# A transformer-like block on one core: keys projected first, diagonal blocks stored by eight small transfers, the delta rule and the attention part moved to earlier places, a new order at the start

## The chip, the cores and the metric

The kernel runs on one core of a Trainium2 chip. The metric is the device time of one execution in microseconds (us); less is better. The time before is the median of three runs, 1259.57 us (1257.01 to 1261.92). The core has five engines that run their own instruction streams and wait for each other by semaphores: TensorE (PE, matrix multiplications), VectorE (DVE), ScalarE (ACT, functions from tables), GpSimd (POOL) and SyncE (SP, which here only issues DMA transfers). ACT issues some transfers too.

## The reference, cut to what matters

One layer for 256 tokens of width 2048, all float32. The token mixer projects the normalised input with one weight, then runs eight heads of stick-breaking attention and eight heads of gated delta rule side by side (head width 128), and projects the result back. A gated MLP with a causal convolution follows. Of the mixer the change touches the order of nearly all steps:

```python
xn = rmsnorm(x, ln_mix_pre)
proj = xn @ w_in                       # sb q,k,v | dn q,k,v | dn z | dn b,a
# stick-breaking, per head and block of 128 queries
z = q @ k.T * 128**-0.5                # log_sigmoid of z and -z, masked
att = exp(log_beta + later)            # later: reversed cumulative sum of log_1m
o_sb = rmsnorm(att @ v, sb_out_gain)
# delta rule, per head; chunks of 64 in the reference
q, k, v = silu(causal_conv4(dn_qkv))   # q and k then l2-normalised
L = where(strict, (k * beta) @ k.T * decay, 0)
T_mat = inverse(I + L)                 # triangular
u, w = T_mat @ (v * beta), T_mat @ (k * beta * exp(g))
# per chunk: v_new = u - w @ S; o = q*exp(g) @ S + qk @ v_new; S = S*exp(g_last) + k.T @ v_new
o_dn = rmsnorm(o_dn, dn_out_gain) * silu(dn_z)
h = x + rmsnorm(concat(o_sb, o_dn) @ w_out, ln_mix_post)
y = h + rmsnorm(conv_ffn(rmsnorm(h, ln_ffn_pre)), ln_ffn_post)
```

## The kernel before, in words

**Precision and weights.** Each float32 weight is split in two parts that PE can take at full speed: `w_hi` (rounded, by ACT, L464) and `w_lo` (the remainder, by DVE, L891); the activations are held in the same two parts (`xhl`, `mix_hl`, `ffn_act`). A product is hi x hi and lo, and lo x hi. Weights come as chunks of 1 MB (`raw`, four slots), issued by SP; a chunk has four pieces of 128x512, and `w_hi` and `w_lo` are rings of eight pieces. A split is made six pieces ahead of PE's use (AHEAD). So ACT and DVE may lag by about six pieces before PE has nothing to do.

**Places.** The input projection is 14 groups of 16 pieces. The first ten give features (`tile_piece`, four tiles of 128 features by 256 tokens, banks 0 to 3); the last four give tokens (`token_piece`). The number of a piece in this order, 0 to 223, is a place. Every engine has a function `follow(place)` that does its share of the stream up to that place: PE the pieces, ACT the splits, the copies of the lower half of a bank (`halves`), the first tap of the convolution and its silu, DVE the splits, the bank additions (`added`) and three taps for each conv tile, POOL the token scale (L346), SP the chunk loads. All other work of the mixer is hung on that stream: the table PLACE gives each step a place, and each engine calls `follow` up to it, then waits for its semaphores and does the step. An engine that waits there makes no splits meanwhile. The program order of each engine is fixed by this.

**The head.** SP loads x in four quarters, each followed by one chunk. ACT issues the gains and four small tensors, then rounds four k-blocks of x (L535), splits the first four pieces, and so on; DVE does the remainders (L934). ACT asks for `xcopy` (x by tokens, 2 MB) after split 5, squares it (L563), takes the root at place 11; DVE makes two diagonals of it (L960) that PE sums at place 14 (L1398) to a scale for each token. At 9 to 12 PE projects the gate columns (`ba`, L1391); DVE, ACT and PE form decays from them at places 15 to 27, and SP stores them and loads them spread over partitions (`dm`).

**Delta rule.** Two batches of four heads, `for b in range(BATCHES)`, hang from places 44 and 115. Keys are turned and their norms taken; `low` is the scaled triangular system in `ltri` (L1028). The diagonal 16x16 blocks are inverted row by row: POOL masks `ltri` to its diagonal blocks (L396), DVE reduces them to `packed` (L1040), SP stores that (64 KB, runs of 512 B for each partition), ACT loads it spread over partitions (`block_l`, L613) at place 58, and DVE works through 15 rows (L1055, L1057) at 66 to 80. POOL spreads the blocks (L401), and three doublings by matmuls (L1434, L1449, L1451) with DVE's additions between (L1070) give the inverse. The outputs and the state follow (L1458).

**Stick-breaking.** Two batches of four heads hang from 186 and 205: `z` matmuls (L1543), on ACT absolute value and exponential (L687, L688) and logarithm (L692), softplus on DVE (L1098), masks on POOL (L366), the matmul with a triangle (L1552), exponential (L698), the matmul with `vtok` (L1563), squares, norm, transposes (L1573). `token_evac` copies the token groups out of their banks at places 176, 192, 208 and 224 (L498); groups 12 and 13 pass through silu. `z_mix`, `z_turn`, `z_hi`, `z_lo` multiply the delta rule's output by its gate and turn it; batch 0 at 212 to 217, batch 1 within the output projection. ACT asks for `out_gain` after the last `sb_hi`; DVE waits for it before its first split of the output projection.

The ScalarE functions come from tables; an ACT_TABLE_LOAD precedes a function of another set.

## Time and profile before

| what | value |
|---|---|
| median of three runs | 1259.57 us |
| the profiled execution | 1259.88 us |
| its span | 1258.0 us, so 1.88 us lie around it |
| PE busy | 1225.7 us, 97% |
| DVE busy | 884.0 us, 70% |
| ACT busy | 737.2 us, 59% |
| POOL busy | 217.7 us, 17% |
| mean granted clock of PE | 0.994 |
| chain that ended last | 94% PE, 2% ACT, 2% DVE, 1% DMA, 1% issue |

A busy share is that of the whole span; where PE is nearly always busy, what is left to find is in the waits of PE and in the stretches with a lower clock. In the rows below a row of the timeline has the start in us, the duration in us of the merged group, the engine, the line of the kernel, the operation, what it writes and reads, the count, and in brackets the idle time before it and what ended that. A matmul of plain float32 counts as two instructions (x2). PEclk is the granted clock of PE as a share of 2.4 GHz.

### The profile page before, as it was taken

Reading aid. Unit: us, or ns where it says so; the run is one execution under the profiler, and the core shown is the slowest. Engines: PE = TensorE matmul, PEld = TensorE weight load, DVE = VectorE, ACT = ScalarE, POOL = GpSimd, SP = SyncE. Lnnn points to the kernel's source line nnn. Section 1 sums busy time; section 2 is a strip of 40 time slices with the busy share of each in tenths; the row PEclk is TensorE's granted clock in tenths of the full one; section 3 lists DMA queues with packets and bytes.
Section 4 is the critical chain, followed back from the end, with each engine's and each line's share of the span. In section 5 each row is a group of like instructions: output and inputs, shape, how many; then the busy total and the mean of one; then the engine's idle time right before and its main releaser. Section 6 shows DMA issues by size and latency. Waiting matters only on the chain.

```text
span 1258.0 us, 20145 instructions
## 1 busy us (share of the span) xinstructions
PE 1225.7 (97%) x6643; PEld 1053.2 (84%) x6643; DVE 884.0 (70%) x1637; ACT 737.2 (59%) x1452; POOL 217.7 (17%) x258
## 2 busy tenths in 40 slices
PE   6999999999998999999999999999999999999997
PEld 4888889888887788788888888888888888888886
DVE  5788976774454655778878888887888875555554
ACT  6776547653677655666566566656656554444442
POOL 1122311232012000022222312322222220000000
PEclk9999999999998999999999999999999999999999
DMA  9565433652333455355555554555545565555551
GB/s 383 201 234 172 177 131 127 199 206 101 134 129 111 173 191 198 132 187 186 196 181 189 193 195 177 185 184 198 200 167 200 198 222 186 196 201 196 185 188 67
DMA packets 33749, 228.91 MB, mean 182 GB/s; under 512 B 4240, under 2 KB 4896, under 8 KB 6944
## 3 DMA queue, kind: packets, MB, share of 16 engines
q1 hardware_dynamic: 31712, 221.40, 49.2%
q10 hardware_dynamic: 1984, 6.81, 1.6%
q8 instruction: 32, 0.52, 0.2%
q14 instruction: 21, 0.17, 0.0%
HBM read 225.96 MB, written 2.24 MB: 181 GB/s over the span
## 4 chain that ended last, share of the span: by engine, by line
PE 94%; ACT 2%; DVE 2%; DMA 1%; issue 1%; POOL 0%; DVEq 0%; SPq 0%; ACTq 0%
PE bank L1334 38%; PE bank L1338 19%; PE bank L1360 10%; PE bank L1362 10%; PE bank L1361 10%; PE bank L1458 1%; PE bank L1434 1%; PE bank L1451 1%; PE bank L1418 1%; DVE w_lo L891 1%; PE bank L1618 1%; PE bank L1617 1%; PE bank L1616 1%; PE bank L1449 1%; DMA raw<-in_wts 1%
## 5 line engine op out<-in xcount | busy, mean ns | idle before, releaser
L891 DVE TENSOR_TENSOR w_lo<-raw,w_hi 128x512 fp32r<-128x512 f32 x816 | 576.3, 729 | 261.3 <-ACT w_hi L464 254.8
L464 ACT ACTIVATE w_hi<-raw 128x512 fp32r<-128x512 f32 x816 | 503.2, 631 | 357.8 <-PE bank L1362 177.8
L1334 PE MATMUL bank<-xhl,w_hi 128*128 128x512 f32 x2048 | 659.3, 399 | 13.1 <-DVE w_lo L891 11.2
L1338 PEld LDWEIGHTS bank<-xhl,w_lo 128*128 128x128 f32 x2048 | 386.2, 189 | 89.0
L1338 PE MATMUL bank<-xhl,w_lo 128*128 128x256 f32 x2048 | 403.7, 278 | 0.0
L1334 PEld LDWEIGHTS bank<-xhl,w_hi 128*128 128x128 f32 x2048 | 317.4, 189 | 15.2 <-issue 12.2
L1360 PE MATMUL bank<-w_hi,ffn_act 128*128 128x512 f32 x336 | 130.7, 389 | 0.0
L1361 PE MATMUL bank<-w_lo,ffn_act 128*128 128x512 f32 x336 | 130.7, 389 | 0.0
L1362 PE MATMUL bank<-w_hi,ffn_act 128*128 128x512 f32 x336 | 130.7, 389 | 0.0
L436 POOL TENSOR_TENSOR arena<-arena,token_scale 128x256 f32<-128x256 f32 x88 | 78.1, 902 | 301.3 <-DVE arena L896 192.3
L1258 DVE SCALAR_TENSOR_TENSOR arena<-arena,fcw 128x256 f32<-128x256 f32 x176 | 85.3, 485 | 23.9 <-DVE arena L1258 1.5
L470 ACT ACTIVATE half<-bank 128x256 f32<-128x256 f32 x128 | 49.6, 387 | 75.6 <-PE bank L1334 74.2
L443 POOL TENSOR_TENSOR ffn_act<-arena,ffn_act 128x256 f32 (+1 forms) x44 | 48.4, 1099 | 168.8 <-ACT ffn_act L815 168.8
L896 DVE TENSOR_TENSOR arena<-bank,half 128x256 f32<-128x256 f32 x128 | 54.0, 422 | 32.5 <-ACT half L470 31.9
L1362 PEld LDWEIGHTS bank<-w_hi,ffn_act 128*128 128x128 f32 x336 | 63.1, 188 | 13.2
L1361 PEld LDWEIGHTS bank<-w_lo,ffn_act 128*128 128x128 f32 x336 | 63.1, 188 | 13.1
L1360 PEld LDWEIGHTS bank<-w_hi,ffn_act 128*128 128x128 f32 x336 | 63.1, 188 | 12.9
L346 POOL TENSOR_TENSOR arena<-arena,token_scale 128x256 f32<-128x256 f32 x40 | 35.0, 886 | 175.2 <-DVE arena L896 139.6
L1360 PE MATMUL bank<-w_hi,xhl 128*128 128x512 f32 x128 | 53.3, 416 | 0.0
L1362 PE MATMUL bank<-w_hi,xhl 128*128 128x512 f32 x128 | 50.4, 394 | 0.0
L1361 PE MATMUL bank<-w_lo,xhl 128*128 128x512 f32 x128 | 50.4, 394 | 0.0
L1360 PE MATMUL bank<-w_hi,mix_hl 128*128 128x512 f32 x112 | 44.3, 396 | 0.0
(235 smaller groups left out, 1011.9 us busy)
## 6 DMA issues: line engine op xcount, KB each, us to landing
raw<-in_wts SPq DMA_DIRECT2D x204, 1024.0 KB, 4.7
xfeat<-in_x SPq DMA_DIRECT2D x4, 512.0 KB, 9.0
arena<-in_x_tok ACTq DMA_DIRECT2D x1, 2048.0 KB, 12.0
xfeat<-in_x_tok SPq DMA_DIRECT2D x1, 2048.0 KB, 11.2
arena<-base_rows ACTq DMA_DIRECT2D x4, 512.0 KB
out_y<-xfeat SPq DMA_DIRECT2D x8, 256.0 KB, 2.0
arena<-gate_rows SPq DMA_DIRECT2D x1, 1024.0 KB, 4.5
arena<-in_post_gains ACTq DMA_DIRECT2D x1, 1024.0 KB, 6.3
```

Of the source, the lines that this page charges most:

```text
L436: pool.tensor_tensor(tile, tile, token_scale[:, 0, :], ALU.mult).then_inc(s("up_scaled"), 1)
L443: pool.tensor_tensor(act[:, k, 1, :].rearrange("p a t -> p (a t)"), prod[:, q % 2, :], act[:, k, 0, :].rearrange("p a t -> p (a t)").bitca ...
L464: nc.scalar.activation(w_hi[:, i % RING, :], raw[:, slot, quarter * PIECE:(quarter + 1) * PIECE], ACT.Copy).then_inc(hi_ready, 1)
L470: nc.scalar.activation(halfs[j % 4], ps[b][:, T:2 * T], ACT.Copy).then_inc(half_ready, 1)
L891: V.tensor_tensor(w_lo[:, i % RING, :], raw[:, slot, quarter * PIECE:(quarter + 1) * PIECE], w_hi[:, i % RING, :].bitcast(f32), ALU.subtra ...
L896: return V.tensor_tensor(out_, ps[b][:, 0:T], halfs[j % 4], ALU.add).then_inc(bank_free, 1)
L1258: ins = V.scalar_tensor_tensor(fconv[:, b, :], src, fcw[:, k, col], fconv[:, b, :], ALU.mult, ALU.add)
L1334: return M(ps[j][:, :], w_hi[:, r % RING, kk * P:(kk + 1) * P], xhl[:, k, :, :].rearrange("p a t -> p (a t)"), start=(k == 0), stop=(k == ...
L1338: return M(ps[j][:, 0:T], w_lo[:, r % RING, kk * P:(kk + 1) * P], xhl[:, CHUNK_K * q + kk, 0, :], start=False, stop=False, skip_group_chec ...
L1360: M(bank[:, :], hl[:, 0, t], w_hi[:, p % RING, :], start=first, stop=False, skip_group_check=True)
L1361: M(bank[:, :], hl[:, 0, t], w_lo[:, p % RING, :], start=False, stop=False, skip_group_check=True)
L1362: ins = M(bank[:, :], hl[:, 1, t], w_hi[:, p % RING, :], start=False, stop=last_, skip_group_check=True)
```

## The change

The weights of the input projection are ordered key, query, value in both delta-rule batches (GROUP_TILE and `weight_chunks`). The four small loads of ACT and the load of `xcopy` are issued later, the latter by SP behind the fourth chunk; the first chunk is loaded in two parts, and the first piece starts as soon as its two k-blocks are there (`first_piece`), behind four matmuls on `ones` (FIRST_WARM). The mask and the reduction to `packed` go; SP stores the eight diagonal blocks out of `ltri` itself, one transfer of 16 partitions x 8 units x 64 B each. The delta rule hangs from 37 and 103, the stick-breaking part from 174 and 199 with other distances within, and the turning of the first gate batch from 217 and 221. The key transposes wait for one silu fewer, the key-query products for the second one.

```diff
-GROUP_TILE = [0, 8, 16, 4, 12, 20, 32, 36, 40, 44]
+GROUP_TILE = [8, 0, 16, 12, 4, 20, 32, 36, 40, 44]
...
-PLACE = {"ba": 9, "stat": 14, "ba_turn": 16, "scale": 15, "gate": 21, "gcum": 24, "grow": 27}
-for _b, _l in enumerate((44, 115)):
+PLACE = {"ba": 10, "stat": 14, "ba_turn": 16, "scale": 15, "gate": 21, "gcum": 24, "grow": 28}
+for _b, _l in enumerate((37, 103)):
     for _g in range(2):
         PLACE["kt", _b, _g] = _l + _g
         PLACE["kk", _b, _g] = _l + 2 + _g
         PLACE["low", _b, _g] = _l + 4 + _g
-        PLACE["qk", _b, _g] = _l + 5 + _g
-        PLACE["qa", _b, _g] = _l + 7 + _g
-        PLACE["mask", _b, _g] = _l + 6 + _g
-        PLACE["pack", _b, _g] = _l + 9 + _g
-        PLACE["qt", _b, _g] = _l + 15 + _g
-        PLACE["vt", _b, _g] = _l + 19 + _g
-        PLACE["spread", _b, _g] = _l + 39
-        PLACE["turn", _b, _g] = _l + 41 + _g
-    PLACE["load", _b] = _l + 14
+        PLACE["qk", _b, _g] = _l + 13 + _g
+        PLACE["qa", _b, _g] = _l + 14 + _g
+        PLACE["qt", _b, _g] = _l + 17 + _g
+        PLACE["vt", _b, _g] = _l + 23 + _g
+        PLACE["spread", _b, _g] = _l + 35
+        PLACE["turn", _b, _g] = _l + 37 + _g
+    PLACE["store", _b] = _l + 6
+    PLACE["load", _b] = _l + 11
     for _i in range(4):
-        PLACE["dm", BH * _b + _i] = _l - 6 + _i
-    PLACE["dexp", _b] = _l - 2
+        PLACE["dm", BH * _b + _i] = _l - 3 + _i
+    PLACE["dexp", _b] = _l + 1
     for _i in range(BASE):
-        PLACE["row", _b, _i] = _l + 21 + _i
+        PLACE["row", _b, _i] = _l + 17 + _i
     for _i in range(2 * LEVELS):
-        PLACE["x", 2 * LEVELS * _b + _i] = _l + 43 + 9 * _i // 4
-        PLACE["y", 2 * LEVELS * _b + _i] = _l + 46 + 9 * _i // 4
-    for _name, _n in (("z0", 59), ("s", 61), ("o0", 61), ("ks", 63), ("qs", 63), ("z1", 65), ("o1", 67), ("rs", 69)):
+        PLACE["x", 2 * LEVELS * _b + _i] = _l + 40 + 9 * _i // 4
+        PLACE["y", 2 * LEVELS * _b + _i] = _l + 43 + 9 * _i // 4
+    for _name, _n in (("z0", 56), ("s", 58), ("o0", 58), ("ks", 60), ("qs", 60), ("z1", 62), ("o1", 64), ("rs", 66)):
         PLACE[_name, _b] = _l + _n
-SB_PLACE = 186
-for _r in range(BATCHES):
-    _s = SB_PLACE + 19 * _r
+SB_PLACE = 174
+for _r, (_s, _c, _a, _o) in enumerate(((174, 9, 18, 23), (199, 9, 14, 19))):
     for _i in range(BH):
         PLACE["z", BH * _r + _i] = _s + _i // 2
         PLACE["sp", BH * _r + _i] = _s + 2 + _i
-        PLACE["c", BH * _r + _i] = _s + 8 + _i // 2
-        PLACE["av", BH * _r + _i] = _s + 12 + _i // 2
-        PLACE["ot", BH * _r + _i] = _s + 17 + _i // 2
+        PLACE["c", BH * _r + _i] = _s + _c + _i // 2
+        PLACE["av", BH * _r + _i] = _s + _a + _i // 2
+        PLACE["ot", BH * _r + _i] = _s + _o + _i // 2
     PLACE["ln", _r] = _s + 4
-    PLACE["norm", _r] = _s + 14
-PLACE["zmix", 0] = 212
-PLACE["zturn", 0] = 215
+    PLACE["norm", _r] = _s + _a + 2
+PLACE["zmix", 0] = 217
+PLACE["zturn", 0] = 221
...
                 sp.dma_start(xfeat[:, 4 * q:4 * q + 4, :], x[:, 4 * q:4 * q + 4, :]).then_inc(s(f"x_in{q}"), 16)
+                if q == 0:
+                    sp.dma_start(raw[:, 0, 0:PIECE], wts[0, :, 0:PIECE]).then_inc(s("first_w"), 16)
+                    sp.dma_start(raw[:, 0, PIECE:CHUNK], wts[0, :, PIECE:CHUNK]).then_inc(raw_full[0], 16)
+                    continue
                 sp.dma_start(raw[:, q, :], wts[q, :, :]).then_inc(raw_full[q], 16)
+            sp.dma_start(xcopy, x_tok).then_inc(s("x_copy_in"), 16)
...
-            follow(10)
+            follow(24)
             sp.wait_ge(s("xn_lo"), KT)
             sp.dma_start(res, x_tok).then_inc(s("x_tok_in"), 16)
...
-                follow(PLACE["pack", b, 1])
-                sp.wait_ge(s("packed"), 2 * b + 2)
-                sp.dma_start(scratch[b], packed.rearrange("p u i -> p (u i)")).then_inc(s("scratch_in"), 16)
+                follow(PLACE["store", b])
+                sp.wait_ge(s("low_ready"), 2 * b + 2)
+                for i in range(NBLK):
+                    rows_ = slice(i * BASE, (i + 1) * BASE)
+                    sp.dma_start(scratch[b].rearrange("p (u i) -> p u i", i=BASE)[rows_], ltri[rows_, :, rows_]
+                                 ).then_inc(s("scratch_in"), 16)
...
-            input_hi(0)
-            for i in range(4):
+            input_hi(0, range(2))
+            split(0, 0)
+            input_hi(0, range(2, 4))
+            for i in range(1, 4):
                 split(0, i)
+            act_e.dma_start(wba[:, :, :], w_ba).then_inc(s("wba_in"), 16)
+            act_e.dma_start(dcw[:, :, :], dn_conv).then_inc(s("small_in"), 16)
+            act_e.dma_start(gate[:, 0:2, :], dn_gate).then_inc(s("gate_in"), 16)
+            act_e.dma_start(hgains[:, :, :], head_gains).then_inc(s("small_in"), 16)
             input_hi(1)
             split(0, 4)
             split(0, 5)
-            act_e.dma_start(xcopy, x_tok).then_inc(s("x_copy_in"), 16)
...
-                if r:
-                    for g in range(2):
-                        z_hi(0, g)
...
+            follow(PLACE["zturn", 0] + 1)
+            for g in range(2):
+                z_hi(0, g)
             act_e.wait_ge(s("av_mm"), HEADS)
             act_e.dma_start(out_gain, post_gains[0, :, :]).then_inc(s("out_gain_in"), 16)
...
+            def first_piece():
+
+                pe.wait_ge(hi_ready, 1)
+                pe.wait_ge(bank_free, 1)
+                for kk in range(0, CHUNK_K, 2):
+                    pe.wait_ge(s("xn_lo"), kk + 2)
+                    for k in (kk, kk + 1):
+                        M(ps[0][:, :], w_hi[:, 0, k * P:(k + 1) * P], xhl[:, k, :, :].rearrange("p a t -> p (a t)"),
+                          start=(k == 0), stop=False, skip_group_check=True)
+                    pe.wait_ge(lo_ready, 1)
+                    for k in (kk, kk + 1):
+                        last = M(ps[0][:, 0:T], w_lo[:, 0, k * P:(k + 1) * P], xhl[:, k, 0, :],
+                                 start=False, stop=False, skip_group_check=True)
+                last.then_inc(piece_used, 1)
...
+            pe.wait_ge(s("const_ready"), 1)
+            for _ in range(FIRST_WARM):
+                M(ps[7][:, :], ones[:, :], ones.rearrange("p (a c) -> p a c", a=1).to_broadcast([P, 4, P]), start=True, stop=True)
...
-                    pe.wait_ge(s("silu_done"), 3 * b + 2)
+                    pe.wait_ge(s("silu_done"), 3 * b + 1)
```

## Rows read from the trace of the kernel before

**Rows 1.** The page: the span, and PE's busy time with its matmuls.
```profile
span 1258.0 us, 20145 instructions
...
PE 1225.7 (97%) x6643; PEld 1053.2 (84%) x6643; DVE 884.0 (70%) x1637; ACT 737.2 (59%) x1452; POOL 217.7 (17%) x258
```

**Rows 2.** Who waited for whom, PE: us in total, times, longest.
```profile
PE bank L1334 <- DVE w_lo L891: 11.2, 2, 9.3
PE bank L1552 <- POOL arena L366: 5.3, 2, 4.6
PE bank L1434 <- issue: 2.0, 1, 2.0
PE bank L1418 <- DVE arena L1107: 1.9, 1, 1.9
```

**Rows 3.** Windows: length, busy (count) per engine, PEclk, DMA share, GB/s.
```profile
0.00:6.00 6.00, 0.00 (x0) 0.00 (x0) 0.33 (x3) 2.16 (x4) 4.42 (x20) 1.00 0.63 213
6.00:22.00 16.00, 12.74 (x59) 11.08 (x60) 9.87 (x20) 8.64 (x20) 1.47 (x5) 1.00 1.02 423
9.20:14.40 5.20, 5.14 (x16) 4.49 (x17) 5.03 (x11) 4.54 (x11) 0.00 (x0) 1.00 1.04 424
14.40:22.80 8.40, 8.40 (x49) 7.29 (x48) 2.81 (x7) 2.58 (x7) 0.00 (x0) 1.00 1.01 428
343.70:353.00 9.30, 9.30 (x41) 7.33 (x40) 2.86 (x6) 8.25 (x16) 0.24 (x1) 1.00 0.34 113
394.60:400.50 5.90, 5.89 (x18) 5.05 (x19) 2.75 (x8) 2.12 (x3) 5.55 (x11) 0.50 0.44 167
431.40:434.40 3.00, 3.00 (x10) 2.31 (x10) 3.00 (x7) 0.84 (x2) 0.00 (x0) 0.50 0.73 216
```

**Rows 4.** Timeline, head: start, us, engine, line, operation.
```profile
27.01 1.90 ACT L563 ACTIVATE arena<-arena 128x2048 f32<-128x2048 f32 x1
...
35.80 0.48 DVE L960 TENSOR_SCALAR arena<-ident,stat 128x128 f32<-128x128 f32 x2
...
38.56 0.59 PE L1398 MATMUL bank<-arena,ones 128*128 128x256 f32 x2
```

**Rows 5.** Timeline, DVE and POOL around the first doubling.
```profile
145.31 3.16 POOL L401 TENSOR_TENSOR arena<-arena 128x512 f32<-128x512 f32 x2
...
145.82 4.36 DVE L912 SCALAR_TENSOR_TENSOR arena<-arena,dcw 128x255 f32<-128x255 f32 x3
...
154.72 1.51 DVE L912 SCALAR_TENSOR_TENSOR arena<-arena,dcw 128x255 f32<-128x255 f32 x3
...
161.69 0.75 DVE L1070 TENSOR_TENSOR arena<-arena,bank 128x256 f32<-128x256 f32 x2
```

**Rows 6.** The store and the loads: issue ns min/median/max, us to landing.
```profile
L613 ACTq DMA_DIRECT2D arena<-base_rows x4: 582/596/1168, 110.6 to 236.6; - x4
L282 SPq DMA_DIRECT2D base_rows<-arena x2: 327/327/327, 108.2 to 234.3; - x2
...
arena<-in_head_gains ACTq DMA_DIRECT2D x1, 128.0 KB, 11.2
base_rows<-arena SPq DMA_DIRECT2D x2, 64.0 KB, 1.5
```

**Rows 7.** Timeline, the stick-breaking batches.
```profile
339.28 0.59 PE L1543 MATMUL bank<-arena 128*128 128x256 f32 x2
...
353.75 0.70 PE L1552 MATMUL bank<-arena 128*128 128x256 f32 x2 [0.73 <-POOL arena L366]
...
382.53 1.28 ACT L498 ACT_TABLE_LOAD   x1
...
393.00 0.55 DVE L1098 SCALAR_TENSOR_TENSOR arena<-bank,arena 128x384 f32<-128x384 f32 x1
```

**Rows 8.** Timeline, the beginning of the out stage.
```profile
420.76 0.33 ACTq L741 DMA_DIRECT2D arena<-in_post_gains  x1
...
427.13 2.50 DVE L891 TENSOR_TENSOR w_lo<-raw,w_hi 128x512 fp32r<-128x512 f32 x4 [4.63 <-DMA arena<-in_post_gains]
```

More of the change, by code:

```diff
@@ L935, in input_lo @@
                                            xhl[:, k, 0, :].bitcast(f32), ALU.mult, ALU.subtract).then_inc(s("xn_lo"), 1)
-            input_lo(0)
-            for i in range(4):
+            input_lo(0, range(2))
+            split(0, 0)
+            input_lo(0, range(2, 4))
+            for i in range(1, 4):
                 split(0, i)
@@ L1036, in _ @@
                                     ).then_inc(s("qa_ready"), 1)
-                for g in range(2):
-                    follow(PLACE["pack", b, g])
-                    dve.wait_ge(s("masked"), 2 * b + g + 1)
-                    V.tensor_reduce(packed[:, 4 * g:4 * g + 4, :],
-                                    tmat[:, 4 * g:4 * g + 4, :].rearrange("p u (b i) -> p u i b", i=BASE),
-                                    mybir.AxisListType.X, ALU.add).then_inc(s("packed"), 1)
                 eye_row = block_row.rearrange("p (a i) -> p a i", a=1).to_broadcast([P, UNITS, BASE])
@@ L1139, in _ @@
                 if r:
-                    for g in range(2):
-                        follow(PLACE["zturn", 0] + 1 + g)
-                        z_lo(0, g)
+                    follow(PLACE["zmix", 0])
+                    z_mix(0)
                 for h in heads:
@@ L1147, in _ @@
                                     ALU.subtract).then_inc(s("sb_lo"), 1)
+            for g in range(2):
+                follow(PLACE["zturn", 0] + 1 + g)
+                z_lo(0, g)
             follow(16 * IN_GROUPS)
@@ L1595, in _ @@
                     sb_av(h)
-                if r:
-                    follow(PLACE["zturn", 0])
-                    pe.wait_ge(s("tok_evac"), 6)
-                    for g in range(2):
-                        z_turn(0, g)
                 for h in heads:
                     sb_ot(h)
+            follow(PLACE["zturn", 0])
+            pe.wait_ge(s("tok_evac"), 6)
+            for g in range(2):
+                z_turn(0, g)
             follow(16 * IN_GROUPS)
@@ L1722, in cols @@
         return w[:, a:a + width]
-    features = [cols(dn, part, b) for b in range(BATCHES) for part in range(3)]
+    features = [cols(dn, part, b) for b in range(BATCHES) for part in (1, 0, 2)]
     features += [cols(sb, part, b) for part in range(2) for b in range(BATCHES)]
```

43 lines of the change are left out of this document (19 added, 24 removed).

## The prediction

> **What bounds the kernel now.** I read the page first, then who waits for whom on PE, then PE's windows, then the timeline around each wait. PE is busy for 1225.7 of 1258.0 us [rows 1], so PE's order of work is the kernel: a change pays only if it shortens the 32.3 us in which PE is idle, or the time in which it runs at half clock. The groups of waits [rows 2] give most of that idle time: 11.2 us for `w_lo` at the head (9.3 of it before the first matmul, 1.9 later), 5.3 us for the mask of the stick-breaking part, 2.0 us at L1434 (the doubling of the triangular inverse), 1.9 us at L1418 (the transposes of the output gate). The windows [rows 3] add the clock: in the stretch from 394.6 to 400.5 us, right behind a wait of 4.6 us, PE is busy at a granted clock of 0.50 (1.2 GHz), and again from 431.4 to 434.4, behind the wait at L1418. At the start the granted clock reads 1.00, but the matmuls tell otherwise: from 9.2 to 14.4 us a busy PE does 16 of them in 5.2 us, from 14.4 to 22.8 it does 49 in 8.4. A feature piece has eight (four high, four low, 3072 columns), so it takes 1.37 to 1.39 us at the later pace and 2.6 at the first; I use 1.39.
>
> **A. The beginning.** Before, PE reaches place 14 (the matmul of the row scale, L1398) at 38.56 [rows 4]. I follow four chains to the same place in the new order.
> DMA: 0.21 MB/us in the first 6 us (1.28 MB), then 0.42 MB/us [rows 3]. `xcopy` now lies behind x and four weight chunks in SP's queue. With the small tensors that is 8.8 MB, landed at 6 + 7.5/0.42 = 24 us. It also stops competing with the last quarter of x, which now has 5.6 MB up to its end and lands near 16.
> ACT (durations read from its timeline, as for all work on ACT and DVE below): the first two k-blocks at 5.2, the first quarter chunk at about 6.1 to 6.8 (before, the whole chunk was awaited until 7.8), the rest in turn; the four small DMA issues now stand behind split 3 and cost about 0.5 us. At 0.42 us a k-block and 0.55 a split, ACT is through split 13 near 21 and waits for `xcopy`.
> PE: four warm-up matmuls of 512 plain fp32 columns. The nearest row is L1398's 256 fp32 columns, 0.59 us at full clock; so 512 take 1.2 us or less warm and at most twice that cold, 4.7 to 9.4 us in all. I take the end at 7.5, about when the first `w_lo` is there. From the second piece on (9.0) PE is not starved: 13 pieces x 1.39 plus four `ba` groups (2048 columns each, so 0.93) bring it to place 14 at 30.8.
> The scale: from the start of the first square (27.01) to the last of the two diagonals (35.80 + 0.48) were 9.3 us [rows 4], all of it ACT and DVE work that the change does not shorten. 24.0 + 9.3 = 33.3. This, not PE, is late last: PE waits 2.5 us for it and goes on at 33.3, which is 5.3 us earlier than before. If `xcopy` lands 2 us later the gain is 3.3; if the scale chain shrank under PE's own time, it is 7.8. Term: **-5.3** (-3.3 to -7.8). It costs nothing later: the gate's wait at place 24 keeps the same neighbours and stays.
>
> **B. The delta rule earlier, without mask and pack.** PE's work is the same; only its waits count. At 161.69 DVE did the additions (L1070) that the next matmul awaited [rows 5]. It was late because at 145.82 three conv steps took 4.36 us as a group instead of 1.51 while POOL spread the base (3.16 us for two), and DVE had come from a row chain threaded with five conv tiles. Rows now lie at 55 to 69 with three conv tiles (55, 65, 69), and two masks on POOL and two reductions on DVE are gone from each batch. From the last row to the first doubling there are 8 places instead of 7. I take the 2.0 us as gone: **-2.0** (0 to -2.0).
> What is new: (1) `dm` must be loaded before place 34 where it had until 38, and DVE, waiting for it, holds its splits back; places 33 to 42 then hold about 17.3 us of DVE work (10 splits of 0.62, 4 conv tiles of 1.5, 1.9 for `dm`, 1.0 for the norm, 2.2 for the low matrices) against 16.6 of PE (10 pieces, and 2.7 for the key matmuls). (2) The second batch begins where the first ends (103 and 103, before 113 and 115), so ACT has squares, two tables and the key copies in four places, some 12.4 us (2.6 + 1.5 + 2.3 + 3.0, four splits, a conv step), against 13.4 of PE for the seven pieces already split and the key matmuls. (3) The store. Low matrices are ready near PE's place 44; the bounds of the store are 8 x 0.33 + 1.5 = 4.1 us (the old store's issue is 0.33, its landing 1.5) and 8 x 1.17 + 11.2 = 20.6 us (the slowest issue of the loads, the slowest small transfer) [rows 6]. I take 5, near the old store, because that row is the same tensor on the same queue. The load then goes out at its place, 48, and lands by 6.3 us later (the 1 MB gain needs that [rows 8]), place 52.5 of 55. So there are about 3.5 us to spare. SP also holds chunk 15 back by 8 issues, which is not wanted before place 54. DVE's and ACT's lead of six pieces (8.3 us) covers each of the three alone; together I give them **+1.0** (0 to +4).
> The Trainium skill bears on (3): "DMA: Bandwidth & Descriptors", Specifications, states that transfers under 512 B make the engine read, modify and write. The new store has runs of 64 B where the old had 512 B. No run here shows such a store; by that page it would lie nearer to the upper bound, which is the last rival below.
>
> **C. The stick-breaking part from 174.** The second batch's z moves from 205 to 199, its mask-dependent matmul from 213 to 208. Before, the token evacuation at place 208, with its own table (1.28 us at 382.53) and a wait for PE, sat between the exponentials, so that the softplus came only at 393.00 [rows 7]. Now 208 comes behind the logarithms. In the first batch, where no other table came between, the chain from the first z (339.28) to the masked matmul (353.75) took 14.5 us [rows 7], 0.7 more than the eight places gave (13.7). Token pieces take 1.36 us (six matmuls; 41 in 9.3 us [rows 3]), so nine places give 15.1. So the 4.6 us go, and with them the half clock behind, 5.9 us at 0.50, which cost half of it: **-7.5** (-4.6 to -7.5 if the wait goes).
> The first batch: nine places instead of eight, but the evacuation of group 10 (1.24 us for two, and the wait for PE at place 176) now falls between its exponentials. Its 0.7 us become about 1.0: **+0.3**. The attention matmul at 192 wants `vtok`, and group 11 is evacuated at place 192 too: the last token half needs PE's piece 191, then 0.65 us. New wait: **+0.8** (0.7 to 1.5).
> At 213 to 221: attention masks behind the gate gain on POOL are done 7 us after place 208 begins, used 10 us after. z_turn at 221 is two places from the first out piece, DVE still has two subtractions: **+0.3** (0 to +1.5).
>
> **D. The out stage.** DVE sat idle 4.63 us until 427.13 for the gain that ACT had asked for at 420.76, and then did z_mix late [rows 8]; PE waited 1.9 us and ran 3.0 us at 0.50. ACT now issues it after z_hi at place 222, before the evacuation of 224, some 4.4 us earlier against PE; with the same 6.3 us to landing it is there 3.2 us into the stage, DVE's four splits and z_mix end at 7.9, wanted at 8.2. **-3.4** (0 to -3.4): 1.9 + 3.0/2.
>
> **Sum.** -5.3 - 2.0 + 1.0 - 7.5 + 0.3 + 0.8 + 0.3 - 3.4 = -15.8. The profiled execution took 1259.88 us, 1.88 more than its span; 1259.9 - 15.8 = 1244.1. The median of the three runs, 1259.57, is 0.3 lower, so I say 1244. Up and down projection are untouched, a full PE at 0.54 of the DMA.
>
> **Rivals.**
> 1. The wait of C moves instead of going: the evacuation at 208 now delays the attention exponential, and PE waits at 213. For it: ACT has two table loads and PE's piece 207 in that chain; against it: ten microseconds of cover. If so, 4.6 + 2.95 come back: 1251.7.
> 2. DVE stays full. The spread (72) and the masks now fall on conv tiles 73, 77, 81, 85 and four bank additions; at 145 POOL made 4.36 us of 1.51 [rows 5]. Then B's 2.0 stay, as much is added in the second batch, and one half-clock stretch of 3 costs: 1244.1 + 2.0 + 2.0 + 3.0 = 1251.1. Against it: this stretch starts with a backlog of under 3 us.
> 3. The new beginning gives only what the earlier first chunk gives, about 1.5, since ACT and not DMA limits it: 1244.1 + 3.8 = 1247.9.
> 4. The store is slow, and the kernel is slower. At 20.6 us the rows begin 13 us late; DVE's lead less its backlog covers 5.6, PE starves 7.4 us, in both batches, each time with 2.95 for the clock: +20.7, less the 1.0 already counted: 1263.8. It decides from a landing 18.6 us behind the first issue; with a landing under 7.6 it costs nothing. For it speak only the small runs and 11.2 us for a small tensor, which was measured with the DMA full (0.42 MB/us).
>
> **How the numbers follow.** Forecast 0.60 (own range 1239 to 1249), rival 1 0.14, rival 2 0.11, rival 3 0.09, rival 4 0.06. Measurement can tell about 0.5%, 6.3 us, from no change. The forecast and rival 3 are faster; rivals 1 and 2 lie 8 us below before and are faster three times in four, else the same; rival 4 is slower, or in part the same. That gives 0.86, 0.09, 0.05. The range takes in rivals 1 to 3 with their spread, 1238 to 1254, and leaves the slow store out.
>
> **What would show it.** A: matmul pairs at 0.70 us spacing from the first piece on, L1398's successor near 33.3 with a PE wait of 2 to 3 us. B: no PE wait between 60 and 200 over 1 us; eight stores that end within 5 us; DVE not waiting at the first row. C: no wait for the mask over 1 us near place 208, granted clock 1.00 there, a wait of 0.8 at place 192. D: no DVE wait for the gain, clock 1.00. The prediction is wrong if PE's idle time is not near 22 us or its half-clock stretches stay.

## The result, and the profile after

The changed kernel takes 1252.82 us (median of 6, 1249.52 to 1253.18), the kernel before 1259.41 (median of 6, 1257.01 to 1261.92): ratio 0.9938, 95% interval 0.9924 to 0.9953. It is faster by 0.6%, 6.6 us. 15.8 us had been forecast.

The page of the kernel after, span and engines, which answers [rows 1]:
```profile
span 1251.1 us, 20175 instructions
...
PE 1226.1 (98%) x6651; PEld 1051.1 (84%) x6651; DVE 877.2 (70%) x1633; ACT 738.8 (59%) x1454; POOL 214.9 (17%) x254
```
PE's busy time includes the new warm-up matmuls, 5.10 us from 1.07. Without them PE does nothing useful for 30.1 us, against 32.3 before: the idle time that was to fall by about ten microseconds fell by 2.2. The rest of the gain is time in which PE worked at half clock.

Who PE waited for, kernel after (us in total, times, longest), beside [rows 2]:
```profile
PE bank L1439 <- DVE arena L1041: 2.8, 1, 2.8
PE bank L1334 <- DVE arena L901: 2.7, 2, 1.6
PE bank L1419 <- DVE arena L967: 2.0, 1, 2.0
PE bank L1334 <- DVE xhl L1184: 1.7, 1, 1.7
PE bank L1455 <- POOL arena L365: 1.7, 2, 1.5
PE bank L1429 <- DVE arena L1001: 1.1, 1, 1.1
...
PE bank L1574 <- POOL arena L372: 0.9, 1, 0.9
PE bank L1585 <- ACT arena L494: 0.9, 1, 0.9
```
The 5.3 us for the mask are 0.9, the waits for the doubling and for the output gate are gone. In the delta rule three waits are new: 2.8 us at L1439 (the transposes of q times k wait for DVE's product, L1041), 2.7 us at L1334 (feature pieces wait for the additions that free their banks, L901), 1.5 us at L1455 (a doubling waits for POOL's masked product, L365).

The head, timeline of the kernel after (start, us, engine, line, operation, [idle before]), beside [rows 4]:
```profile
25.41 1.91 ACT L566 ACTIVATE arena<-arena 128x2048 f32<-128x2048 f32 x1 [2.85 <-DMA arena<-in_x_tok]
...
34.21 0.47 DVE L967 TENSOR_SCALAR arena<-ident,stat 128x128 f32<-128x128 f32 x2
...
34.84 0.67 PE L1419 MATMUL bank<-arena,ones 128*128 128x256 f32 x2 [2.02 <-DVE arena L967]
```
Place 14 comes at 34.84 instead of 38.56.

Places 42 to 54, timeline of the kernel after, the first store and load of the diagonal blocks:
```profile
84.99 5.17 SPq L287 DMA_DIRECT2D base_rows<-arena  x8
...
92.71 1.80 ACTq L616 DMA_DIRECT2D arena<-base_rows  x2
...
94.85 1.15 ACT L464 ACTIVATE w_hi<-raw 128x512 fp32r<-128x512 f32 x2 [5.53 <-issue]
95.52 0.69 DVE L896 TENSOR_TENSOR w_lo<-raw,w_hi 128x512 fp32r<-128x512 f32 x1 [4.78 <-ACT w_hi L464]
...
100.19 0.68 DVE L1041 TENSOR_TENSOR arena<-bank,arena 128x512 f32<-128x512 f32 x1
...
100.93 0.66 PE L1439 MATMUL bank<-ident,arena 128*128 128x128 f32 x4 [2.75 <-DVE arena L1041]
```
The row of SP is eight issues in 5.17 us. The DMA part of the page gives their landing, beside [rows 6] (KB each, median us from issue to landing):
```profile
base_rows<-arena SPq DMA_DIRECT2D x16, 8.0 KB, 1.8
```
The store is quick, but ACT, which issues the load, does no arithmetic for 5.53 us (89.3 to 94.85): first it waits for the last store, then it issues the two loads. `w_hi` is late, then DVE, then PE.

The length of this stand changes between executions. Of nine kept traces in which this stretch has the same steps (this one, `old_beginning`, `second_at_106`, `second_at_109`, `second_masks_early`, `old_attention_places`, `late_out_gain`, `no_warm_up`, `stat_at_15`), seven have ACT without arithmetic for 3.95 to 4.24 us here and PE waiting 1.3 to 1.5 us; this one has 5.53 and 2.75, `late_out_gain` 6.07 and 3.3. From the timeline of `no_warm_up`:
```profile
93.57 1.15 ACT L464 ACTIVATE w_hi<-raw 128x512 fp32r<-128x512 f32 x2 [4.24 <-PE bank L1334]
99.65 0.65 PE L1439 MATMUL bank<-ident,arena 128*128 128x128 f32 x4 [1.52 <-DVE arena L1041]
```
The stores' issue takes 5.16 us there too; the slowest of them lands after 1.9 us, where it is 3.1 in the kernel after and 3.7 in `late_out_gain`. So 2.8 us is the high end of this wait and 1.5 its usual size.

Around the second batch's keys, timeline of the kernel after:
```profile
199.50 1.28 ACT L595 ACT_TABLE_LOAD   x1
...
203.95 0.69 DVE L896 TENSOR_TENSOR w_lo<-raw,w_hi 128x512 fp32r<-128x512 f32 x1 [3.74 <-ACT w_hi L464]
...
207.95 1.12 DVE L1035 SCALAR_TENSOR_TENSOR arena<-bank,arena 128x128 f32<-128x128 f32 x4
...
211.22 0.41 DVE L901 TENSOR_TENSOR arena<-bank,half 128x256 f32<-128x256 f32 x1
...
211.78 0.47 PE L1334 MATMUL bank<-xhl,w_hi 128*128 128x512 f32 x1 [1.65 <-DVE arena L901]
```
From 194.07 to 205.3 ACT does the first batch's squares and root, the second batch's exponential and key copies, with two table loads and three splits between; DVE then still has norms, splits and the low matrices ahead of the addition at 211.22.

PE's windows of the kernel after (length, busy, clock, DMA share, GB/s), at the two places that ran at 0.50 [rows 3], and the one slice of 20 us that is under 1.00 ahead of the last:
```profile
395.00:401.00 6.00, 6.00 (x41) 1.00 0.47 175
425.00:431.00 6.00, 6.00 (x30) 1.00 0.56 190
500.00:520.00 20.00, 17.75 (x94) 0.91 0.14 53
```
Both half-clock stretches are gone. 0.91 over 20 us is 3.6 us at half clock, which cost 1.8; before had 1.00 there. It lies behind a wait of 1.71 us for the second stage's input (509.33; 517.63 in the kernel before), in code that the change doesn't touch. All fourteen kept traces have that wait and eleven of them a half-clock stretch behind it; the kernel before, `second_at_106` and `stat_at_15` have none. So these 1.8 us are not shown to be an effect of the change.

### The profile page after: what moved, and what is told of

The parts are those of the page before. It is cut to its first block, busy times and chain, and to the rows that moved or that the text cites. A ratio compares the mean times of both kernels' runs of the same rounds, so it can differ in the third digit from the quotient of the medians.

```text
span 1251.1 us, 20175 instructions
## 1 busy us (share of the span) xinstructions
PE 1226.1 (98%) x6651; PEld 1051.1 (84%) x6651; DVE 877.2 (70%) x1633; ACT 738.8 (59%) x1454; POOL 214.9 (17%) x254
## 4 chain that ended last, share of the span: by engine, by line
PE 85%; DVE 5%; ACT 3%; DMA 3%; issue 2%; POOL 1%; SPq 1%; DVEq 0%; ACTq 0%; POOLq 0%
PE bank L1334 32%; PE bank L1338 16%; PE bank L1362 10%; PE bank L1360 10%; PE bank L1361 10%; DVE w_lo L896 2%; DMA arena<-in_x_tok 2%; DMA arena<-base_rows 1%; DVE arena L917 1%; PE bank L1479 1%; ACT w_hi L464 1%; PE bank L1472 1%; PE bank L1455 1%; PE bank L1639 1%; PE bank L1637 1%
## 5 line engine op out<-in xcount | busy, mean ns | idle before, releaser
L1334 PE MATMUL bank<-xhl,w_hi 128*128 128x512 f32 x2044 | 659.7, 399 | 5.4 <-DVE arena L901 2.7
L1334 PEld LDWEIGHTS bank<-xhl,w_hi 128*128 128x128 f32 x2044 | 317.1, 189 | 7.3 <-DVE w_lo L896 3.3
L901 DVE TENSOR_TENSOR arena<-bank,half 128x256 f32<-128x256 f32 x128 | 53.9, 421 | 32.5 <-ACT half L470 32.0
L1255 DVE TENSOR_SCALAR arena<-arena,fcw,fcb 128x256 f32<-128x256 f32 x88 | 45.4, 516 | 0.0
```

The source lines that it names most:

```text
L901: return V.tensor_tensor(out_, ps[b][:, 0:T], halfs[j % 4], ALU.add).then_inc(bank_free, 1)
L1334: return M(ps[j][:, :], w_hi[:, r % RING, kk * P:(kk + 1) * P], xhl[:, k, :, :].rearrange("p a t -> p (a t)"), start=(k == 0), stop=(k == ...
```

## The experiments

Twelve kernels, each timed in five rounds beside the kernel before (medians of 1259.76 to 1260.03 in the four groups). All start from the changed kernel. Their ratios to before, with intervals of 0.0009 to 0.0014 either way, compare with 0.9938; differences under about 0.0020 (2.5 us) are not told apart.

**Undoing the beginning** (`old_beginning`).
```
-PLACE = {"ba": 10, ...
+PLACE = {"ba": 9, ...
-                if q == 0:                                 # the first chunk in two
-                    sp.dma_start(raw[:, 0, 0:PIECE], wts[0, :, 0:PIECE]).then_inc(s("first_w"), 16)
...
-            sp.dma_start(xcopy, x_tok).then_inc(s("x_copy_in"), 16)      # SP, behind x
+            act_e.dma_start(xcopy, x_tok).then_inc(s("x_copy_in"), 16)   # ACT, behind split 5
...
-            for _ in range(FIRST_WARM):
```


> The changed kernel with the old beginning (order of the first transfers, xcopy asked for by ACT, whole first chunk, no first_piece, no warm-up matmuls, ba at 9, grow at 27, res at 10); the rest as changed. Theory: the new beginning is worth the 3.7 us by which the row-scale matmul came earlier (38.56 to 34.84), and later waits do not depend on it. Then the time is 1252.8 + 3.7 = 1256.5 us, and the waits at 98 to 101 and at 211 stay, 3.7 us later. Rival: ACT and DVE enter place 34 with less lead because PE is earlier, so part of the gain is given back in the delta rule; then undoing it costs under 2 us (below 1254.8) and the wait on L1041 shrinks.


1254.44 us, ratio 0.9960 (0.9947 to 0.9974). Part A is worth 1.6 us by the medians, 2.8 by the ratios; 5.3 had been forecast. The time is the rival's (below 1254.8). Its other sign, a smaller wait for L1041, is there too (1.5 us), but most executions with the new beginning have 1.5 as well, so it tells nothing. The profiled execution was the slowest of the six (1257.33): place 14 comes at 40.87 in it, with a clock of 0.83 from 20 to 40 us. So a half-clock stretch in the head can come with the old beginning too.

**Loads from SP** (`load_by_sp`).
```
-                follow(PLACE["load", b])                       # ACT
-                act_e.wait_ge(s("scratch_in"), 16 * NBLK * (b + 1))
-                    act_e.dma_start(block_l[:, rows_]...
+                sp.wait_ge(s("scratch_in"), 16 * NBLK * (b + 1))   # SP, right behind the stores
+                    sp.dma_start(block_l[:, rows_]...
```


> The changed kernel, with the two loads of the spread blocks issued by SP right behind its stores instead of by ACT at place 48; ACT no longer waits for the stores. Theory: PE's 2.75 us at 98 to 101 come from ACT, which stood 5.5 us (89.3 to 94.85) at the load's place, in order, for the eight stores (5.2 us of issue, 1.8 to 3.1 to landing) and then issued for 1.8 us; without that the PE wait goes and DVE's wait for the blocks (1.48) stays or shrinks: 1252.8 - 2.75 = 1250.0, in both batches ACT idle before w_hi under 1.5 us there. Rival: DVE is behind by its own work (conv tiles 49, 51 next to qa at 51), the wait stays above 2 us and the time within 1 us of 1252.8.


1260.05 us, ratio 1.0003 (0.9994 to 1.0012). Timeline of this kernel:
```profile
93.21 1.34 SPq L294 DMA_DIRECT2D arena<-base_rows  x2
94.60 25.21 SPq L270 DMA_DIRECT2D raw<-in_wts  x6
...
108.72 0.63 ACT L473 ACTIVATE w_hi<-raw 128x512 fp32r<-128x512 f32 x1 [11.16 <-DMA raw<-in_wts]
```
The wait for L1041 is gone, so ACT's stand at the loads was its cause; but now SP stands there. The next weight chunk is issued at 94.60, 2.9 us behind the end of the stores' issue, where the kernel after issues it right behind them (90.20), and lands behind the loads, 14.1 us after its issue; PE then waits 7.4 us. Neither side of the expectation had this wait. It is what the forecast should have priced for a wait on either queue: who is queued behind it.

**Loads two places later** (`load_at_plus_13`).
```
-    PLACE["load", _b] = _l + 11
+    PLACE["load", _b] = _l + 13
```


> The loads of the stored inverses are put two places later in ACT's order (place l + 13 instead of l + 11), so ACT makes two more splits of raw weights before it waits for the stores to land. My theory: TensorE's wait of 2.75 us at 100.93 us (L1439 for DVE's L1041) comes from ACT standing in order at the loads while the high half of a weight piece is not made; with two splits more ahead of the loads it falls under 0.5 us, the time is 2 to 3 us under the changed kernel's, about 1250.0 us against 1252.8. DVE's wait for base_rows at its first row grows by what the loads are later, and doesn't reach TensorE. Rival: DVE is the full engine there, and the wait moves to the rows of the system or to the first output of the delta rule: a wait of 2 to 3 us for DVE or POOL after 105 us, time within 1 us of 1252.8.


1252.79 us, ratio 0.9943 (0.9929 to 0.9956). From the waits of PE, this kernel:
```profile
PE bank L1439 <- POOL arena L399: 1.1, 1, 1.1
```
Its window of PE right behind place 14, and, from its timeline, the gate's matmul:
```profile
34.00:40.00 6.00, 5.21 (x21) 0.72 0.59 213
```
```profile
52.54 0.36 PE L1429 MATMUL bank<-arena 128*128 128x16 f32 x2 [1.15 <-DVE arena L1001]
```
The wait for L1041 is gone from the trace, as the theory wants; 0.9 us come back at L1439 for POOL's spread (0.2 in the kernel after), and the median doesn't move. Against the usual 1.5 us of that wait there were only some 0.6 us to gain. The last two rows show why a profile of one execution misleads here: the same instructions and the same wait of 2.0 us at 34.8 are followed by matmuls at half clock in this execution and not in the one of the kernel after (L1429 at 52.54, there at 51.03). 1.5 us went that way. Whether the removed wait is worth something in the median stays open within 2 us.

**The second batch at 106 and at 109** (`second_at_106`, `second_at_109`).
```
-for _b, _l in enumerate((37, 103)):
+for _b, _l in enumerate((37, 106)):     # the other kernel: (37, 109)
```


> The changed kernel with the second delta-rule batch hung from 106 instead of 103, all else as changed. Theory: PE's 2.74 us at 211 to 214.5 (for the bank additions of DVE) come from the two batches meeting at 103: ACT does squares, root, exponential and key copies from 194 to 205 and DVE waits for it. Three places (4.2 us) apart, the wait falls under 0.5 us: 1252.8 - 2.3 = 1250.5. Rival: the wait is DVE's total load there (low matrices, conv tiles at 105 and 109, bank additions at 109 to 112), then low at 110 and 111 falls on the additions and the wait stays or grows: 1252.8 to 1254.

> The second batch of the delta rule begins at place 109 instead of 103. My theory: the 2.74 us of TensorE's waits for DVE's bank additions near 212 to 215 us (L1334 for L901) come from the key and low-half work of the new batch that stands on DVE ahead of the additions of the group that ends at place 110; at 109 that work stands behind them, the waits fall under 1 us in sum, and the time is about 1250.5 us. Rival: the six places are then missing at the batch's end, just ahead of the attention's first step at 174, and the wait is made up by waits for POOL or DVE at 335 to 345 us (after has 0.9 us there): 3 us or more there and a time of 1252.8 us or over.


At 106: 1253.94 us, ratio 0.9955 (0.9943 to 0.9967). The waits for L901 are 3.2 us in four: the low matrices now lie between the additions, and the time is the rival's. At 109: 1261.35 us, ratio 1.0015 (1.0006 to 1.0024). Waits of PE at 109:
```profile
PE bank L1334 <- DVE arena L901: 5.5, 3, 2.7
PE bank L1574 <- POOL arena L372: 3.2, 1, 3.2
```
My theory fell: the waits doubled. ACT's exponential (208.53), key copies (210.28 to 216.6) and the first silu then stand between the very pieces whose additions PE awaits, and the batch ends too late for the attention's first mask, as the rival said. 109 is the worse place; 103 and 106 are not told apart.

**The second batch's exponential early** (`second_masks_early`).
```
-                follow(PLACE["dexp", b] - 1)             # 103, both batches in their own loop
+                if b == 0: ... dm[:, 0:4] as before
...
+                if b == 0:                               # DVE at 92 and 93, ACT at 95
+                    act_e.wait_ge(s("ddiff"), HEADS)
+                    nc.scalar.activation(dm[:, BH:HEADS, :], dm[:, BH:HEADS, :], ACT.Exp)
```


> The decay exponents of the second batch (eight DVE tensor_scalar of 0.2 us and ACT's exponential with its table load, 2.3 us) are made at places 92 to 95, before the first batch ends, instead of at 100 to 103; nothing else moves. Theory: TensorE's waits for DVE's bank additions (L901 in the changed kernel, 2.74 us in two at 211.8 and 214.5) come from ACT's unbroken burst at places 102 to 108: output squares, root, exponential, key copies, root, with three table loads; 3.6 us of it go (the exponential, its table and the reload of the root's), the waits fall under 0.7 us in sum, and the time is 2 to 2.5 us under the changed kernel's: about 1250.5. Rival: DVE's own order at that point (key norms and low halves right ahead of the additions) holds them whatever ACT does: the waits stay at 2 us or more and the time within 0.7 us of 1252.8.


1252.91 us, ratio 0.9948 (0.9936 to 0.9961). Waits of PE:
```profile
PE bank L1494 <- DVE arena L1096: 2.1, 1, 2.1
...
PE bank L1349 <- DVE arena L907: 0.6, 1, 0.6
```
L907 is the addition (L901 before the edit). Its waits fell from 2.7 to 0.6, so the early burst was their cause, and DVE's order of norms and additions, which stayed, was not. The edit also takes 1.6 us of DVE's work (the exponents' subtractions) out of the same stretch; that ACT's part decides and not DVE's is read from the trace of the kernel after, where DVE, behind that work, still stood idle 3.74 us for `w_hi` (203.95). But the exponential and its table, 2.3 us on ACT at 181.3, made the first batch's key product (L1096) 2.1 us late: the wait moved. The wait went as the theory said, the time as the rival did.

**The old places of the attention** (`old_attention_places`).
```
-SB_PLACE = 174
-for _r, (_s, _c, _a, _o) in enumerate(((174, 9, 18, 23), (199, 9, 14, 19))):
+for _r, (_s, _c, _a, _o) in enumerate(((186, 8, 12, 17), (205, 8, 12, 17))):
```


> The changed kernel with the stick-breaking part back at its old places and inner distances (186 and 205; 8, 12, 17), the rest as changed. Theory: the mask wait of 4.6 us near place 213 with its half-clock stretch of 5.9 us comes back, and the 0.9 at 192 goes: 1252.8 + 7.5 - 0.9 = 1259.4, plus up to 1 more for the gate turning that now comes behind place 223. Rival: the wait before came from the state of ACT as it arrived, not from the places: the time stays under 1256.


1262.38 us, ratio 1.0025 (1.0014 to 1.0037): 9.6 us slower than the changed kernel and 2 to 3 above what the theory gave. Waits of PE, and its windows:
```profile
PE bank L1574 <- POOL arena L372: 5.3, 2, 4.6
PE bank L1360 <- DVE mix_hl L1117: 3.1, 1, 3.1
```
```profile
380.00:400.00 20.00, 15.42 (x64) 0.83 0.32 116
420.00:440.00 20.00, 16.86 (x72) 0.91 0.61 212
```
The wait for the mask and the half clock behind it return. The wait at the out stage is another one than before's. From the timeline of this kernel:
```profile
420.34 0.33 ACTq L746 DMA_DIRECT2D arena<-in_post_gains  x1
422.08 1.29 DVE L1117 TENSOR_TENSOR mix_hl<-bank,mix_hl 128x512 fp32r<-128x512 f32 x2
423.43 0.79 PE L1360 MATMUL bank<-w_hi,mix_hl 128*128 128x512 f32 x1 [3.13 <-DVE mix_hl L1117]
428.23 2.50 DVE L896 TENSOR_TENSOR w_lo<-raw,w_hi 128x512 fp32r<-128x512 f32 x4 [4.86 <-DMA arena<-in_post_gains]
```
PE waits for the first gate batch, whose low part DVE makes late here (L1117), and goes on at 423.43, ahead of the gain row. The row is as late as before, since ACT's last attention step now stands at place 224, ahead of the request (asked for at 420.34, awaited by DVE until 428.23), but PE, held up by its own wait and the half clock behind it, doesn't wait for what follows the row. So this run prices C and D together, with a wait of 3.1 us in it that neither of the two kernels has; it doesn't separate them.

**The gain row asked for late** (`late_out_gain`).
```
+            follow(16 * IN_GROUPS)
             act_e.wait_ge(s("av_mm"), HEADS)
             act_e.dma_start(out_gain, post_gains[0, :, :])...
```


> The gain row of the output stage is asked for only after place 224, as a load that ACT issues late; the rest is the changed kernel. This undoes the last part alone. Theory (the prediction's D): its early issue took away a wait of TensorE near 427 us with a stretch at half clock behind it; undone, a wait of about 2 us for DVE at L1117 comes back, PEclk shows a slice under 0.95 at 420 to 440 us, and the time is 3 to 3.5 us above 1252.8, about 1256. Rival: the row was late only because of what else stood on ACT's queue before; the time stays within 0.7 us of 1252.8.


1254.53 us (1251.94 to 1256.24), ratio 0.9952 (0.9938 to 0.9966), 1.7 us above the changed kernel: between theory and rival, and told apart neither from nothing nor from the forecast 3.4. Timeline of this kernel:
```profile
416.90 1.28 ACT L494 ACT_TABLE_LOAD   x1
418.99 0.33 ACTq L747 DMA_DIRECT2D arena<-in_post_gains  x1
423.76 2.50 DVE L897 TENSOR_TENSOR w_lo<-raw,w_hi 128x512 fp32r<-128x512 f32 x4 [5.12 <-ACT w_hi L464]
427.45 0.63 PE L1440 MATMUL bank<-ident,arena 128*128 128x128 f32 x4 [0.30 <-DVE arena L1109]
```
and the same steps in the kernel after:
```profile
412.06 0.33 ACTq L746 DMA_DIRECT2D arena<-in_post_gains  x1
414.10 1.28 ACT L494 ACT_TABLE_LOAD   x1
418.15 3.04 DVE L896 TENSOR_TENSOR w_lo<-raw,w_hi 128x512 fp32r<-128x512 f32 x4 [2.30 <-DMA arena<-in_post_gains]
```
The row is asked for 2.1 us behind the start of the stage's table load instead of 2.0 us ahead of it, and DVE stands idle 5.12 us instead of 2.30. The bracket names `w_hi`, but ACT had made the four pieces by 422.4; what came at 423.7 is the row, 4.7 us after its issue. From DVE's start behind the row to PE's matmul it is 3.7 us here (423.76 to 427.45), as in the kernel before (427.13 to 430.83), where the row took 6.3 us. So the chain that the prediction named for D is back and has used up all the slack, but PE waits only 0.3 us, because the row landed faster; with 6.3 us it would have waited about 1.9 (my estimate: 0.3 + 6.3 - 4.7), which is before's wait. The clock reads 1.00 from 400 to 440. The same execution has 3.3 us for L1042 (L1041 before the edit) and 0.91 at 100 to 120 us, which the edit doesn't touch; it is the slowest of the five (1256.24).

**The head** (`no_warm_up`, `stat_at_15`).
```
-FIRST_WARM = 4
+FIRST_WARM = 0                                            # no_warm_up
-..."stat": 14, "ba_turn": 16, "scale": 15, "gate": 21, "gcum": 24
+..."stat": 15, "ba_turn": 16, "scale": 16, "gate": 21, "gcum": 25   # stat_at_15
```


> The eight matmuls over a buffer of ones ahead of the first real one are left out (they compute nothing that is used). Theory: the granted clock of the first real matmuls is at its lower level for some 4 us more than in the changed kernel, the first real matmul begins at 7.0 us as before, and the time is 1.5 to 2.5 us above 1252.8. Rival: the first stretch waits for the transfers and the input's halves anyway, with gaps in which a slower TensorE costs nothing: the time stays within 0.7 us of 1252.8.

> The head's token sums move one place (14 to 15, with their scale at 16) and the cumulative gate from 24 to 25; nothing else moves. Theory: TensorE's waits of 2.02 us for x_diag at 34.84 and of 1.14 us for the gate at 51.03 go by one piece of matmuls each (1.38 us), so 2.5 us, and with the first of them the half-clock stretch that stood behind it in some executions (0.91 at 20 to 40 us in the profiles of load_at_plus_13 and second_at_109, 1.5 us); time 1249.5 to 1250.5. Rival: the token scale is now late for POOL and through it for later work, or the gain is made up by a wait later in the head: time within 0.7 us of 1252.8.


Without warm-up: 1251.54 us, ratio 0.9940 (0.9926 to 0.9953). The warm-up buys nothing; my theory fell. The wait for the diagonals of the row scale (L967) was 1.3 us instead of 2.0: the slow first pieces used up time that PE would have waited. Token sums at 15: 1251.09 us, ratio 0.9933 (0.9921 to 0.9945), the fastest median of all, but within the interval of 0.9938. The waits in the head are 0.6 + 0.5 + 0.9 + 0.7 us where they were 2.0 + 1.1; those for L901 grew from 2.7 to 3.9. The time lies between the theory's and the rival's.

**Several at once** (`all_mended`, `four_mended`).
```
# all_mended: second_masks_early + stat_at_15 + load_at_plus_13 + no_warm_up, and
-                follow(PLACE["x", i] - 2)                 # POOL's level_b
+                follow(min(PLACE["x", i] - 2, PLACE["x", i - r] - 1) if r < 3 else PLACE["x", i] - 2)
-((174, 9, 18, 23), ...
+((174, 9, 19, 24), ...
# four_mended: exponents at 87 (DVE) and 90 (ACT), "stat" 15 with "gcum" 24, load at l + 12, FIRST_WARM = 0
```


> Everything that the waits of the changed kernel point to at once: the two changes above, the loads of the inverses two places later, no warm-up matmuls, POOL's mask products of the first levels ahead of its token scales, and the first attention round's products with their norms and outputs one place later. Theory: each wait was TensorE's alone and their gains add: 2.7 (L901) + 1.9 (L1041, less what L399 takes) + 2.5 (head) + 1.5 (L365) + 0.9 (L494) + 1 (warm-up) = 10.5 us at most under 1252.8; with what stays hidden, 1243 to 1245. Rival: DVE and ACT are near full in the stretches at 85 to 145 and 195 to 215 us, so that a wait that is taken away comes back at the next thing they owe: no more than half of it is gained, 1247.5 or more.

> Four of the mends that earlier runs measured, without those that brought a wait of their own: the second batch's decay exponents now at places 87 and 88 on DVE and at 90 on ACT (second_masks_early had them at 92 to 95, right ahead of the first batch's key product, where ACT's table load and exponential made a new wait of 2.13 us for L1096), token sums at 15, the loads one place later (12), no warm-up. Theory: at place 90 ACT stands idle 0.8 to 1.6 us between pieces, so the 2.3 us are hidden there and the wait for L1096 goes; against stat_at_15 (1251.1) the waits for L901 fall from 3.9 to under 1, the one for L1041 from 1.3 to under 0.7, the warm-up gives about 1: 1246.5 to 1248.5 us. Rival: ACT has no 2.3 us anywhere between 85 and 100, and L1096 or another wait of 1.5 to 2 us comes back: 1249.5 or more.


1254.92 us, ratio 0.9964 (0.9952 to 0.9976), and 1253.00 us, ratio 0.9943 (0.9931 to 0.9955). Both rivals held. Waits of PE, `four_mended`:
```profile
PE bank L1445 <- DVE arena L1008: 2.3, 1, 2.3
...
PE bank L1471 <- POOL arena L366: 1.7, 2, 1.5
PE bank L1455 <- POOL arena L400: 1.1, 1, 1.1
```
The waits for L1041 are gone and those for the additions and the key product are 0.6 each, but the gate's wait (L1001 there, L1008 here) grew from 1.1 to 2.3, with 0.91 for the clock from 40 to 60 us, and POOL's grew by 0.9. PE's idle time is 26.1 us, against 26.6 in `no_warm_up`. So no version beat the changed kernel by more than can be measured.

## Why the prediction was right in its sign and too large in its size

**A, the beginning: -5.3 forecast, -3.7 in the trace, -1.6 (medians) or -2.8 (ratios) by its undoing.** The scale chain took 9.3 us, as forecast (25.41 to 34.68), and it was late last, with PE waiting 2.0 us of the 2.5. `xcopy` landed at 25.4 or a little before, not at 24.0: the 8.8 MB at 0.42 MB/us were short by 1.4 us. What else the undoing lacks is not shown. The clock may be part of it: before, PE ran without a wait from 27.87 to its wait for the gate; now a wait of 2 us stands at 34.8, and 0.72 from 34 to 40 us followed it in the profiles of `load_at_plus_13` and `load_by_sp`, 1.5 us each. But the profile of `old_beginning` has 0.83 from 20 to 40 us. The forecast priced the wait at its length alone.

**B, the delta rule: -1.0 forecast, +4 to +5 in fact. This is the step that failed.** The -2.0 for the doubling held, except that another doubling, at 141.44, waits 1.5 us for POOL. The "+1.0" for what is new is the mis-sized term: it measured 2.75 (L1041) + 2.74 (L901) + 1.7 (L365) = 7.2 us in the kernel after, and about 5.9 with the 1.5 us that L1041 costs in most executions. Of its three items, `dm` brought no wait. The store took 7.7 us from the first issue to the last landing (84.99 to 92.71; 6.4 in `no_warm_up`) against 5 taken, since an issue took 0.6 us and not the old store's 0.33; that is far from the 20.6 of rival 4, but it kept ACT standing 1.4 to 2.7 us longer. The Trainium skill's page "DMA: Bandwidth & Descriptors", Specifications, states that transfers under 512 B make the engine read, modify and write. The prediction took from it that the store would lie nearer the upper bound; this trace doesn't bear that out: the eight landed in 1.8 us at the median and 3.1 at most, against 1.5 for the old one and 11.2 in the bound. What was wrong is the sentence that six pieces of lead (8.3 us) cover each of the three alone. The load was given a landing and a price for who reads it, and none for who stands in its queue: ACT waits there in order from 89.3 to the last landing and issues for 1.8 us more, not long behind a stretch that I had myself found full (17.3 us of DVE work against 16.6 of PE). And the second batch's burst on ACT was laid against 13.4 us of PE as if all of the lead were free; but a bank addition has only three places (4.2 us) between the piece that fills the bank and the piece that wants it back. The cover of a bank is not the cover of the weight ring. `second_masks_early` shows the burst as cause of the second wait, `load_by_sp` and `load_at_plus_13` ACT's stand as cause of the first. That POOL's token scales, which wait in order for the additions (the scale at 139.07 stood idle 4.80 us for L901, the product at 139.95 behind it), are the cause of the third is read from the trace; `all_mended`, which reordered them, had a wait of 2.0 us at the next doubling instead.

**C and D: -9.5 forecast together, -9.9 in the trace, -9.6 by undoing the places of the attention (-11 by the ratios).** The masked matmul waits 0.9 (forecast 1.0), place 192 waits 0.9 (forecast 0.8), rival 1 didn't come. D's wait is gone too, and what the prediction said of its cause stands: in the kernel before DVE stood for the row until 427.13 and PE's matmul followed 3.7 us later; in `late_out_gain` the late row brings that chain back, 3.7 us again. What is not shown is its price: 0.3 us in the one trace of the late row, about 1.9 if the row had landed as slowly as before, and a median that tells neither from the other. The early row itself comes from the attention's earlier places: ACT's last attention step (the copy at place 220) now comes ahead of the request at 222, where before it stood at 224 and took the request behind the last evacuation. So `old_attention_places` has the row late again as well. That the two sums agree (9.5 and 9.6) is in part luck, since the undoing holds a wait of 3.1 us with its half clock that is not before's.

Sum by the undoings: -2 for A, -10 for C and D, which leaves about +5 for B, that was not undone by itself, to give the measured -7; by the trace -3.7 + 5.2 - 9.9 + 1.8 (the clock at 500 to 520) = -6.6. Of the 9 us missed, 5 to 6 are B's and 1.6 to 3.7 A's; the trace adds 1.8 of the clock at 500 to 520.

Rivals 1 and 2 came nearest in time (1251.7 and 1251.1) and neither happened: the mask's wait did not move to 213, and the doubling at L1434 did not stay late for the spread. Rival 2 had the right stage, though: both batches of the delta rule cost PE 2 to 3 us. Rival 3 gave the size of A but not its reason, since ACT did wait 2.85 us for the transfer.

## What to carry to other kernels

A wait that is put on an in-order engine costs everything queued behind it: price the queue, for each engine that could hold it (here 1.3 to 3.3 us on ACT, 7.4 on SP), and count a cover per resource, since the shortest one (three places of a bank) decides, not the longest. A chain read from one trace has to be followed to the engine that pays: the late gain row cost DVE 5.1 us of idle time in one run and PE 0.3. And one trace of an undoing is not its price: between executions the row's landing ranged from 4.7 to 7.9 us and that of the slowest of the first eight stores from 1.9 to 3.7, which is as much as these waits. Near a full PE, removing single waits of 2 us moved them to the next thing owed and gave nothing that five rounds could tell.

## What the runs showed that I had not expected

- Stores with runs of 64 B were not slow: eight of 8 KB were issued in 5.17 us (0.56 to 0.69 each, against 0.33 for the old one) and landed 1.8 us after issue at the median, 3.1 at most (3.7 in `late_out_gain`). The slowest one decides, since the load waits for all eight: PE's wait behind it was 1.3 to 1.5 us in seven traces and 2.8 and 3.3 in the two with the late landing.
- A weight chunk issued 1.4 us behind the two loads, which spread 1 MB over the partitions, landed after 14.1 us and starved ACT for 11.16.
- After the same wait of 2.0 us at 34.8 the clock fell to its lower level in four traces (`load_by_sp`, `load_at_plus_13`, `second_at_109`, `late_out_gain`: 0.91 from 20 to 40 us) and stayed at 1.00 in four others of the same instructions. A stretch at 0.91 over 20 us cost 1.5 to 1.8 us, as much as most of the waits tested here.
- Eight warm-up matmuls, 5.10 us, brought nothing (1251.54 without, 1252.82 with).
